# Score rows split over two PSUM banks by tile parity, with the low queries' product in two halves of 64 rows

## What is computed

```python
s_c = einsum(q, k_c) * scale      # 63 compressed keys, one per 16 tokens
s_s = einsum(q, k_g) * scale      # selected blocks (here all of the causal ones)
s_w = einsum(q, k_wb) * scale     # sliding window of 512 tokens
p_* = masked_softmax(s_*, mask)
o   = gate_c * p_c @ v_c + gate_s * p_s @ v_s + gate_w * p_w @ v_w
```

## Time and profile before

| | |
|---|---|
| median of three runs | 665.57 us (665.19 to 665.87) |
| the profiled execution | 665.02 us |
| its span | 663.2 us |
| PE busy | 653.1 us, 98% |
| DVE busy | 487.0 us, 73% |
| ACT busy | 377.7 us, 57% |
| POOL busy | 200.8 us, 30% |
| granted clock, mean | 1.00 |

### The profile page before, as it was taken

How to read it: one execution, slowest core, us unless ns; L and a number is a source line. 1 busy time by engine, 2 the same in 40 slices (tenths; PEclk the granted TensorE clock), 3 DMA queues, 4 the chain that set the end, 5 groups by cost and what they waited for, 6 DMA issues and landing times.

```text
span 663.2 us, 10318 instructions
## 1 busy us (share of the span) xinstructions
PE 653.1 (98%) x3513; PEld 551.7 (83%) x3513; DVE 487.0 (73%) x1152; ACT 377.7 (57%) x872; POOL 200.8 (30%) x220
## 2 busy tenths in 40 slices
PE   9999999999999999999999999998999999999998
PEld 6889998888888888888888888886878888888886
DVE  5956989986747655775797876888887778787853
ACT  6754458554435444555565665767775655555651
POOL 3433304433423232321312312158532221211210
PEclk9999999999999999999999999999999999999999
DMA  8413202202111111101101100143111011011101
GB/s 316 150 56 113 64 1 65 64 17 64 47 49 33 36 44 33 39 26 33 33 16 33 33 17 26 39 127 127 64 48 50 32 49 48 32 45 39 45 33 64
DMA packets 20212, 37.35 MB, mean 56 GB/s; under 512 B 2880, under 2 KB 4288, under 8 KB 20160
## 3 DMA queue, kind: packets, MB, share of 16 engines
q1 hardware_dynamic: 20016, 36.68, 17.2%
q10 hardware_dynamic: 144, 0.00, 0.0%
HBM read 32.48 MB, written 4.19 MB: 55 GB/s over the span
## 4 chain that ended last, share of the span: by engine, by line
PE 87%; DVE 9%; ACT 2%; issue 1%; ACTq 0%; DVEq 0%
PE pf L1451 10%; PE pf L1452 10%; PE pf L1453 10%; PE tp L1761 8%; PE sc L1605 5%; PE sc L1604 4%; PE po L1741 4%; PE po L1742 4%; PE pj L1453 4%; PE pj L1452 4%; PE pj L1451 4%; PE sc L1451 3%; PE sc L1453 3%; PE sc L1452 3%; DVE sc L1358 2%
## 5 line engine op out<-in xcount | busy, mean ns | idle before, releaser
L952 ACT CAST pth<-tp 128x512 fp32r<-128x512 f32 (+1 forms) x148 | 86.8, 587 | 122.4 <-PE tp L1761 121.8
L1358 DVE CUSTOM_DVE_ANT_0 sc<-sc,maskb 128x64 f32<-128x64 f32 (+8 forms) x192 | 103.1, 561 | 47.2 <-PE sc L1605 46.3
L1380 DVE TENSOR_TENSOR ptl<-tp,pth 128x512 fp32r<-128x512 f32 x132 | 91.0, 690 | 30.5 <-ACT pth L952 30.2
L672 POOL TENSOR_SCALAR qp<-qp,precip,gate 128x64 f32<-128x64 f32 x64 | 41.4, 647 | 192.6 <-DVE precip L1348 192.4
L1761 PE MATMUL tp<-cst,qp 128*128 128x128 f32 (+1 forms) x592 | 88.9, 273 | 0.5 <-issue 0.2
L632 POOL TENSOR_TENSOR fl<-fraw,fh 128x512 fp32r<-128x512 f32 x40 | 54.1, 1352 | 101.4 <-ACT fh L797 101.4
L1451 PE MATMUL pf<-hh,fh 128*128 128x512 f32 x200 | 80.4, 402 | 2.3 <-DVE th L1318 1.6
L1452 PE MATMUL pf<-hl,fh 128*128 128x512 f32 x200 | 78.4, 392 | 0.0
L1453 PE MATMUL pf<-hh,fl 128*128 128x512 f32 x200 | 78.1, 391 | 0.0
L1761 PEld LDWEIGHTS tp<-cst,qp 128*128 128x128 f32 (+1 forms) x592 | 68.6, 137 | 11.2 <-issue 1.5
L623 POOL TENSOR_TENSOR wl<-qp,wh 128x512 fp32r<-128x512 f32 (+1 forms) x33 | 49.3, 1516 | 87.4 <-ACT wh L712 83.8
(11 more groups left out here) (256 smaller groups left out, 1556.2 us busy)
## 6 DMA issues: line engine op xcount, KB each, us to landing
fraw<-in_wside SPq DMA_DIRECT2D x40, 256.0 KB, 2.6
qp<-in_wpack SPq DMA_DIRECT2D x28, 256.0 KB, 3.1
xo<-in_x SPq DMA_DIRECT2D x16, 256.0 KB, 2.5
out<-xo SPq DMA_DIRECT2D x16, 256.0 KB, 2.1
wor<-in_wout SPq DMA_DIRECT2D x12, 256.0 KB, 2.8
mixc<-in_xcm SPq DMA_DIRECT2D x4, 512.0 KB, 7.1
xlow<-in_xcm SPq DMA_DIRECT2D x3, 512.0 KB, 5.9
qp<-in_wpack SPq DMA_DIRECT2D x5, 224.0 KB, 2.6
```

What stands on the lines that cost most here:

```text
L952: nc.scalar.copy(pth[ptn % 2][0:r, :], tp[tpn % 2][0:r, :]).then_inc(pth_ready, 1)
L1358: return V.tensor_tensor_reduce(row, row, mask, -1.0, -NEG, ALU.add, ALU.min, most)
L1380: V.tensor_tensor(ptl[ptn % 2][:, :], tp[tpn % 2][:, :], pth[ptn % 2][:, :].bitcast(F32), ALU.subtract).then_inc(tp_read, 1)
```

## The change

Key tiles with an even number keep high keys in rows 0 to 63 and low keys in rows 64 to 127; in odd tiles the halves are swapped. For selected rows from tile 4 on and window rows from tile 3 on, the key tiles of the query tile's own parity ("own") go to the second bank and the others to the first. The high queries still take the whole height of 128 rows, in one product per bank. The low queries take only the rows where the high keys lie: rows 0 to 63 for one parity, rows 64 to 127 for the other, in two products of 64 rows, each into its own bank. Low x low is no longer computed there. In these window rows the compressed keys get two products of their own, of 128 rows and 64 columns, ahead of the others. The order of tiles in the row changes, so the mask of the window's oldest tile moves and the transposes look up their tile's place. The copy of the diagonal tile and its wait are gone from tile 3 on. `key_lo` makes two instructions of 256 columns, one for each half of the rows.

```diff
+def sel_split(i):
+    return i >= 4
+def win_split(i):
+    return i >= 3
+def sel_order(i):
+    own, other = range(i % 2, i + 1, 2), range(1 - i % 2, i + 1, 2)
+    return [*other, *own] if sel_split(i) else list(range(i + 1))
+def win_order(i):
+    tiles = range(max(0, i - WT), i + 1)
+    return sorted(tiles, key=lambda j: j % 2 == i % 2) if win_split(i) else list(tiles)
 def sel_column(i):
-    n = i + 1
-    return 0 if n <= 4 else 512 - (n + 1) // 2 * P
+    return 512 - (i + 1) // 2 * P if sel_split(i) else 0
 def win_column(i):
-    return end_column(i) - min(i, WT) * P
+    return 512 - 2 * P if win_split(i) else 0
+def cmp_column(i):
+    return win_column(i) - CB if win_split(i) else (i + 1) * P
...
-                if u is not None and u >= 2:
+                if u is not None and u >= 2 and not win_split(UNITS[u][0]):
                     copy_last_keys(u)
...
             def key_lo(n, dst):
                 dve.wait_ge(kt_hi, n + 1)
-                V.tensor_tensor(dst, xt[n % 2][HD:P, :], dst.bitcast(F32), ALU.subtract).then_inc(kt_ready, 1)
+                for odd in range(2):
+                    rows = slice(0, HD) if odd else slice(HD, P)
+                    low = dst[rows, :].rearrange("p (t u c) -> p u t c", u=2, c=P)[:, odd]
+                    both = xt[n % 2][rows, :].rearrange("p (t u c) -> p u t c", u=2, c=P)[:, odd]
+                    ins = V.tensor_tensor(low, both, low.bitcast(F32), ALU.subtract)
+                ins.then_inc(kt_ready, 1)
...
+            def by_row_groups(row, b, g, i, j0, h, with_blocks):
+                def tiles(parity):
+                    js = range(j0 + (parity - j0) % 2, i + 1, 2)
+                    return len(js) * P, kst[:, b, g, :].rearrange("p (t u c) -> p u t c", u=2, c=P)[:, parity, js[0] // 2:js[-1] // 2 + 1, :]
+                def span(lo, hi):
+                    return row[:, lo:hi].rearrange("p (t c) -> p t c", c=P)
+                own, other = i % 2, 1 - i % 2
+                hi_rows = [slice(0, HD), slice(HD, P)]
+                n_own, k_own = tiles(own)
+                n_other, k_other = tiles(other)
+                to_own, to_other = span(512, 512 + n_own), span(512 - n_other, 512)
+                c = 512 - n_other - CB
+                if with_blocks:
+                    keys_times(row[:, c:c + CB], kend[:, g, P:P + CB], h)
+                MM(to_other, qh[:, h, :], k_other, start=True, stop=False)
+                MM(to_own, qh[:, h, :], k_own, start=True, stop=False)
+                MM(to_own, ql[hi_rows[own], h, :], k_own[hi_rows[own]], start=False, stop=True)
+                return MM(to_other, ql[hi_rows[other], h, :], k_other[hi_rows[other]], start=False, stop=True)
...
-                if h == 0 and w % 2 == 1:
+                if h == 0 and w % 2 == 1 and not win_split(i):
                     pe.wait_ge(kend_ready, w // 2 + 1)
...
                 if w % 2 == 0:
-                    o, n = sel_column(i), i + 1
-                    first = min(n, 4 - o // P)
-                    for a, b in ((0, first), (first, n)):
-                        if a < b:
-                            ins = keys_times(s[:, o + a * P:o + b * P], kst[:, 0, g, a * P:b * P], h)
+                    if sel_split(i):
+                        ins = by_row_groups(s, 0, g, i, 0, h, False)
+                    else:
+                        ins = keys_times(s[:, 0:(i + 1) * P], kst[:, 0, g, 0:(i + 1) * P], h)
+                elif win_split(i):
+                    ins = by_row_groups(s, 1, g, i, max(0, i - WT), h, True)
                 else:
-                    o, e, j0 = win_column(i), end_column(i), max(0, i - WT)
-                    if j0 < i:
-                        keys_times(s[:, o:e], kst[:, 1, g, j0 * P:i * P], h)
-                    ins = keys_times(s[:, e:e + P + CB], kend[:, g, :], h)
+                    if i:
+                        keys_times(s[:, 0:i * P], kst[:, 1, g, 0:i * P], h)
+                    ins = keys_times(s[:, i * P:(i + 1) * P + CB], kend[:, g, :], h)
```

More of the change, by code:

```diff
@@ L130, in job_tiles @@
     return [("w", j) for j in range(max(0, i - WT), i + 1)] + [("c", 0)]
+def sel_split(i):
[8 more added lines that the diff above has]
+    return sorted(tiles, key=lambda j: j % 2 == i % 2) if win_split(i) else list(tiles)
 def sel_column(i):
-    n = i + 1
-    return 0 if n <= 4 else 512 - (n + 1) // 2 * P
-def end_column(i):
-    return 512 if i >= 3 else i * P
+    return 512 - (i + 1) // 2 * P if sel_split(i) else 0
 def win_column(i):
-    return end_column(i) - min(i, WT) * P
+    return 512 - 2 * P if win_split(i) else 0
+def cmp_column(i):
+    return win_column(i) - CB if win_split(i) else (i + 1) * P
 def turns_at(k):
@@ L220, in halves_at @@
     return out
-WIDE_STEP = next(k for k in range(NS) if k // 4 % 2 and end_column(UNITS[k // 8][0]) == 512)
+WIDE_STEP = next(k for k in range(NS) if k // 4 % 2 and win_split(UNITS[k // 8][0]))
 EARLY = (SIDE_AT[2 * (WIDE_STEP - 2)]) // 8
@@ L938, in exponentials @@
                 else:
-                    e = end_column(i)
-                    A(cmp_probs(i, h), sc[s % 2][:, e + P:e + P + CB], ACT.Exp, scale=-1.0,
+                    c, o = cmp_column(i), win_column(i)
+                    A(cmp_probs(i, h), sc[s % 2][:, c:c + CB], ACT.Exp, scale=-1.0,
                       bias=nmax[:, s % 4, 1:2], accum_out=psums[:, s % 4, 1:2])
-                    A(win_probs(i, h), sc[s % 2][:, win_column(i):e + P], ACT.Exp, scale=-1.0,
+                    A(win_probs(i, h), sc[s % 2][:, o:o + (min(i, WT) + 1) * P], ACT.Exp, scale=-1.0,
                       bias=nmax[:, s % 4, 0:1], accum_out=psums[:, s % 4, 0:1]).then_inc(exp_done, 1)
@@ L1205, in keys_lo @@
                 for n in (first, first + 1):
-                    key_lo(n0 + n, kst[HD:P, b, n // 2, (n % 2) * 512:(n % 2 + 1) * 512])
+                    key_lo(n0 + n, kst[:, b, n // 2, (n % 2) * 512:(n % 2 + 1) * 512])
             def positions(f):
@@ L1367, in maxima @@
                 else:
-                    e = end_column(i)
-                    masked_maxima(sc[s % 2][:, e + P:e + P + CB], blocked[:, i, :], nmax[:, s % 4, 1:2])
-                    masked_maxima(sc[s % 2][:, win_column(i):e + P], banded if i >= WT else causal(i + 1),
+                    c, o = cmp_column(i), win_column(i)
+                    masked_maxima(sc[s % 2][:, c:c + CB], blocked[:, i, :], nmax[:, s % 4, 1:2])
+                    masked_maxima(sc[s % 2][:, o:o + (min(i, WT) + 1) * P], banded if i >= WT else causal(i + 1),
                                   nmax[:, s % 4, 0:1]).then_inc(max_ready, 1)
@@ L1754, in turn @@
                     if kind == "s":
-                        src = sel_probs(i, h)[:, j * P:(j + 1) * P]
+                        c = sel_order(i).index(j)
+                        src = sel_probs(i, h)[:, c * P:(c + 1) * P]
                     elif kind == "w":
-                        c = j - max(0, i - WT)
+                        c = win_order(i).index(j)
                         src = win_probs(i, h)[:, c * P:(c + 1) * P]
@@ L1815, in mask_constants @@
     m[:, B_SEL + SEQ - P:B_SEL + SEQ] = near
-    m[:, B_WIN:B_WIN + P] = np.where(k > r, 0, NEG)
+    m[:, B_WIN + 2 * P:B_WIN + 3 * P] = np.where(k > r, 0, NEG)
     m[:, B_CMP - P:B_CMP] = near
```

## The result

The changed kernel takes 683.21 us in the median of four runs (682.96 to 683.43), the kernel before 665.54 beside it: a ratio of 1.0263, interval 1.0251 to 1.0275, 17.7 us slower. The direction is the one forecast and the time lies inside the range of 661.8 to 688.0, but the size was forecast as 6.1 us; the measured one is nearly three times that, and it is nearer to the rival *emptying at the tail's full price* (685.4 us). The time lies in the range only because the range was drawn wide enough to take in that rival; the forecast's own range ended at 676.

The account below looks back on a forecast made before the run. PE, busy 98% of the span, was taken to bound the kernel. Window steps of tiles 4 to 7 +4.8, tile 3 +1.2 and key halves +0.1 gave +6.1 us, 671.6 us; range 661.8 to 688, forecast's own 667 to 676.

Parts of the forecast that it names:

- emptying at the tail's full price: Rival: each of 144 height switches shows a 0.16 us tail, low products overlapping; +19.8 us, 685.4 us; chance 0.20.
- the floor of 0.11 us: PE products: narrow ones cost about 0.11 us start to start whatever their width, read as the weight load.
- The strided key reads: Products over tiles of one parity read 128-column runs with gaps: cost 0; otherwise 17 us over 288 products.
- the first rival: Free overlap: both low products start together and switches are free; net -3.2 us, 662.4 to 663.4 us; chance 0.21.
- the two costs that the trace does not show: Score steps: whether two 64-row products overlap, and the price of switching between full and half height, 144 times.
- 144 switches at 0.06 us: Two height switches in each of 72 steps: 8.6 us, about giving back an overlap worth 9.3 us.
- my upper bound: Price of one height switch at most: tail 0.16 us plus bare weight load 0.11, together 0.27 us.
- a row on active columns: Trace row: four transposes with 64 active columns between full products take 0.67 us, a shape change costing 0.
- the no-overlap case: Score steps: half-height products don't overlap and switches are free; +6.1 us, inside the forecast case of chance 0.44.
- A sign that I had named for a wrong forecast: Score steps: the forecast is wrong if each step shows 0.3 us or more of gap.
- the two extra narrow products: Window steps, compressed keys' own products: +0.15 us a step, +4.8 us for tiles 4 to 7, +1.2 for tile 3.
- the key halves: DVE makes low keys in two 256-column instructions instead of one of 512: +0.1 us, at most 0.8.

Follow-up runs that it names:

- e_full_low: The changed kernel with both low products over all 128 rows again instead of 64; 671.14 us against 665.85 for the kernel before, ratio 1.0080.
- e_same_rows: The changed kernel with both low products on rows 0 to 63, still into two banks; 692.05 us, ratio 1.0395 to the kernel before.

## Why the prediction was right in direction and wrong in size

What held: PE's stream is the time. The start-to-start prices, with the floor of 0.11 us, gave a window step of 0.81 us without half-height products (0.80 in e_full_low). The strided key reads cost nothing. The overlap of the first rival is there, and more than I gave it (10.4 us instead of 9.3): I let the second low product's weights come 0.11 us after the first's, but the two loads run at the same time (both at 622.62).

The step that failed is the one on the two costs that the trace did not show, "I take that overlap, if there is any, is about given back by the switches: 144 switches at 0.06 us". A change of height costs 0.16 to 0.20 us, three times that, so the overlap was not given back but paid for more than twice over. I had the two parts of the price in my upper bound, an array that must be empty (I took the tail, 0.16; the gap is 0.10) and a weight load that comes bare (0.11; it is 0.10 ahead of a low product, 0.055 ahead of a transpose). I gave the first alone to one rival and both together to another, and took for the forecast a value far below either, for no better reason than a row on active columns and that the number then came out the same as in the no-overlap case. That was a choice by convenience. The row on columns was nearer than nothing, but it is about a change that leaves the rows alone. A sign that I had named for a wrong forecast came true: 0.3 us or more a step.

By measured prices: the changed kernel and e_full_low run the same 3,593 products in the same order, so their traces can be laid side by side. The 72 steps are 9.9 us longer up to their transposes, and the first transposes behind them 4.0 us (0.055 each): 13.9 us. In that the overlap has already given back the shorter low product of each step, which is 0.12 us in tile 4's and all window steps, 0.175 in tile 5's and 6's, 0.23 in tile 7's selected ones: 8 x 0.70 + 40 x 0.12 = 10.4 us. So the changes of height cost 24.3 us, 0.34 us a step, where the sum of rounded rows above has 0.36. Outside the steps the changed kernel is 2.4 us shorter, in about a dozen places; 1.2 of it are five waits of PE for DVE that shrink or vanish. That leaves 11.5 us between the two profiled executions; the medians differ by 12.1.

The stretch in which DVE nearly binds, the steps of tile 5, in e_full_low and in the changed kernel (length; busy PE, PEld, DVE, ACT, POOL; clock, DMA share, GB/s):

```profile
439.80:503.80 64.00, 61.57 (x344) 52.22 (x343) 53.37 (x119) 46.76 (x105) 36.68 (x35) 1.00 0.31 99
```

```profile
444.00:509.60 65.60, 63.62 (x342) 49.04 (x341) 53.30 (x119) 46.40 (x104) 36.18 (x35) 1.00 0.30 97
```

DVE's work is the 53.3 us of the earlier trace rows, within 0.1, in all three; PE's idle time falls from 2.7 us before to 2.4 and 2.0 as its own stream grows.

Smaller terms: the two extra narrow products were priced at +6.0 us and the key halves at +0.1. Together they measure 5.3 in e_full_low. The products' term is right: the steps grow by 6.1 us there. The halves' term is not. A half does take nearer to half (0.42 us against 0.69), but I let PE's waits grow by 0.1 us, at most 0.8, and they grew from 0.2 to 1.5 us.

The rival *emptying at the tail's full price* came within 2.2 us with 685.4, by half of the mechanism. It had the gap at each change but kept the loads hidden, and the 0.16 us that it gave to the gap alone happens to be close to what gap and bare load cost together (0.17 in the mean): its nearness is in part luck. The Trainium skill, TensorEngine Tiling, "Key Properties", says that a change of tiling mode drains the engine. The trace agrees in that 0.10 us go by at each change in which PE does nothing, ahead of a load that no longer runs early; what the array does in them no row shows. And the Trainium skill, TensorE: Matmul & The Clock Gate, "Measured speedup vs the span model", puts the issue of each further tile packed into the array at about 4 ns; the trace has the two starts 3 to 4 ns apart.

## What to carry to other kernels

Half-height products on distinct rows and in two banks do run at the same time, but entering and leaving that form costs about 0.34 us here, as much time as full-height products need for some 750 columns (an estimate from 0.232 us for 512). It pays only if that much streaming is saved per visit, so gather many such products between two changes or leave them out; gathering was not tried here. When a cost has no row, price its parts (here the gap and the bare load) and add them, and don't settle on a middle value because two cases then agree. And look for runs of narrow products, of 64 to 192 columns here: each costs its weight load, 0.11 us, and merging four into two is the only change here that made the kernel faster, by 1.1 us.

## What the runs showed of the hardware that was not expected

The price of a change of height is the same both ways between score products of 512 columns, 0.20 us, made of 0.10 us in which neither side of PE does anything and 0.10 us of bare load; into a transpose it is 0.16. A second product of the same height on the same rows pays neither (e_same_rows). On distinct rows the weight loads run at the same time too, not only the products. And one engine can hide this in its own totals: PE's busy share rose from 98% to 99% while it did less work a microsecond, since a product's record covers its load; only the idle time ahead of the weight loads (16.2 us at L1650) gave it away.
